# The second shift's row tiles: from TensorE to ScalarE and GpSimd

## The reference

```
mod = c @ w_ada + b_ada                      # w_ada: 2048 x 12288
sh1, sc1, gt1, sh2, sc2, gt2 = split(mod, 6)
h    = rmsnorm(x, g_mix) * (1 + sc1) + sh1
proj = h @ w_in                              # 2048 x 5376; attention and retention on its columns
x    = x + gt1 * (concat(attention, retention) @ w_out)
h2   = rmsnorm(x, g_ffn) * (1 + sc2) + sh2
x    = x + gt2 * (square(relu(h2 @ w1)) @ w2)
out  = rmsnorm(x, g_final)
```

## Time and profile before

| | us |
|---|---|
| median of 3 runs | 1198.6 (1196.89 to 1198.94) |
| the profiled execution | 1198.73 |
| its span in the trace | 1196.9 |
| TensorE busy | 1128.5 (94%) |
| VectorE busy | 808.2 (68%) |
| ScalarE busy | 490.6 (41%) |
| GpSimd busy | 19.1 (2%) |

### The profile page before, as it was taken

One profiled execution on the slowest core, in us unless ns is written; L12 is line 12 of the kernel. 1 busy time (PEld: TensorE's weight loads), 2 busy tenths in 40 slices (PEclk: granted clock), 3 DMA queues, 4 the chain that ended last, 5 costly groups with the idle time before them and its releaser, 6 DMA issues.

```text
span 1196.9 us, 15614 instructions
## 1 busy us (share of the span) xinstructions
PE 1128.5 (94%) x6235; PEld 963.2 (80%) x6235; DVE 808.2 (68%) x653; ACT 490.6 (41%) x495; POOL 19.1 (2%) x23
## 2 busy tenths in 40 slices
PE   0489999999999999999999999999999999999996
PEld 0489989888778778888888888888888888888884
DVE  5877767988776978875656566655656555665675
ACT  2233444554543445444333444333444333444442
POOL 2000001000000000100000000000000000000000
PEclk9779999999999999999999999999999999999998
DMA  9999988899997866767666667666666665665541
GB/s 363 402 331 332 361 295 296 317 363 385 354 407 298 293 218 234 233 189 266 225 235 187 186 190 255 239 217 200 185 205 245 217 240 182 188 194 182 190 155 71
DMA packets 152250, 302.94 MB, mean 253 GB/s; under 512 B 5088, under 2 KB 73296, under 8 KB 143632
## 3 DMA queue, kind: packets, MB, share of 16 engines
q1 hardware_dynamic: 150880, 298.08, 71.4%
q10 hardware_dynamic: 832, 2.93, 0.6%
q0 software_dynamic: 496, 1.35, 0.3%
HBM read 300.24 MB, written 2.10 MB: 253 GB/s over the span
## 4 chain that ended last, share of the span: by engine, by line
PE 87%; DVE 8%; DMA 3%; issue 1%; ACT 0%; ACTq 0%; DVEq 0%; SPq 0%
PE ps_job L765 18%; PE ps_job L800 14%; PE ps_job L802 14%; PE ps_job L801 14%; PE ps_job L768 9%; PE ps_job L780 4%; PE ps_job L781 4%; PE ps_job L782 4%; DVE acc L1045 3%; DVE w_lo L1105 2%; PE ps L864 1%; DMA stage<-in_w_ada 1%; DMA gate_rows<-in_w_ada 1%; PE ps L742 1%; DMA cst<-in_consts 1%
## 5 line engine op out<-in xcount | busy, mean ns | idle before, releaser
L1105 DVE TENSOR_TENSOR w_lo<-stage,w_hi 128x2048 fp32r<-128x2048 f32 x186 | 426.2, 2291 | 244.2 <-ACT w_hi L453 244.1
L453 ACT ACTIVATE w_hi<-stage 128x2048 fp32r<-128x2048 f32 x186 | 356.1, 1915 | 512.4 <-PE ps_job L802 309.4
L765 PE MATMUL ps_job<-act_hl,w_hi 128*128 128x512 f32 x1024 | 322.2, 396 | 2.3 <-DVE w_lo L1105 1.6
L768 PEld LDWEIGHTS ps_job<-act_hl,w_lo 128*128 128x128 f32 x1024 | 192.4, 188 | 45.4
L768 PE MATMUL ps_job<-act_hl,w_lo 128*128 128x256 f32 x1024 | 201.2, 278 | 0.0
L800 PE MATMUL ps_job<-w_hi,hid_hl 128*128 128x512 f32 x512 | 200.8, 392 | 0.0
L801 PE MATMUL ps_job<-w_lo,hid_hl 128*128 128x512 f32 x512 | 199.3, 389 | 0.0
L802 PE MATMUL ps_job<-w_hi,hid_hl 128*128 128x512 f32 x512 | 199.2, 389 | 0.0
L765 PEld LDWEIGHTS ps_job<-act_hl,w_hi 128*128 128x128 f32 x1024 | 156.1, 189 | 3.3 <-issue 1.8
L1045 DVE SCALAR_TENSOR_TENSOR acc<-stage,small,acc 128x2048 f32<-128x2048 f32 x64 | 150.3, 2348 | 5.7 <-DMA stage<-in_w_ada 2.6
L801 PEld LDWEIGHTS ps_job<-w_lo,hid_hl 128*128 128x128 f32 x512 | 96.1, 188 | 20.8 <-issue 1.0
(11 more groups left out here) (170 smaller groups left out, 788.4 us busy)
## 6 DMA issues: line engine op xcount, KB each, us to landing
stage<-in_w SPq DMA_DIRECT2D x128, 1024.0 KB, 5.4
stage<-in_w_ada SPq DMA_DIRECT2D x80, 1024.0 KB, 7.2
stage<-in_w_in SPq DMA_DIRECT2D x42, 1024.0 KB, 6.3
stage<-in_w_out SPq DMA_DIRECT2D x16, 1024.0 KB, 8.4
gate_rows<-in_w_ada SPq DMA_DIRECT2D x16, 1024.0 KB, 7.1
x_sb<-in_x ACTq DMA_DIRECT2D x1, 2048.0 KB, 14.2
out_y<-f_acc SPq DMA_DIRECT2D x3, 512.0 KB, 4.3
acc<-in_g_final POOLq DMA_DIRECT2D x1, 1024.0 KB, 7.4
```

Of the source, the lines that this page charges most:

```text
L453: nc.scalar.activation(w_hi[:, ring, :], stage[:, slot, :], ACT.Copy).then_inc(hi_ready, 1)
L765: nc.tensor.matmul(ps_job[:, 2 * pair + e, :], w_hi[:, ring, ws], act_hl[:, kt, :], start=(kt == 0), stop=False)
L768: last = nc.tensor.matmul(ps_job[:, 2 * pair + e, T:2 * T], w_lo[:, ring, ws], act_hl[:, kt, 0:T], start=False, stop=(kt == KT - 1))
L1105: nc.vector.tensor_tensor(w_lo[:, ring, :], stage[:, slot, :], w_hi[:, ring, :].bitcast(F32), ALU.subtract).then_inc(lo_ready, 1)
```

## The change

The row tiles no longer pass through TensorE one pair at a time. For each, ScalarE multiplies the tile in place in its slot by its values of c (`scale_row`, an ACTIVATE of 128x2048), and GpSimd adds the slot to an accumulator of its own, `row_acc` (a TENSOR_TENSOR of 128x2048, both inputs in SBUF). `scale_row` stands in ScalarE's program right ahead of the rounding of the group that follows the row tile. After g55 TensorE sums `row_acc` over its rows as it sums the others, with 16 matmuls.

The row tiles move in the list: before, two stood ahead of g29, g31, and so on to g43; now one stands ahead of each of g23, 24, 26, 28, 30, 32, 33, 35, 37, 39, 41, 42, 44, 46, 48 and 50. They are called r0 to r15 below. They count in `lo_ready` no more: a slot that held a row tile is free when GpSimd has added it (`row_added`), and SyncE waits for that.

```diff
-PRE = 5 * KT
+PRE = 4 * KT
+ROW_GROUP = [G_B + 4 + (G_MLP - G_B - 10) * k // KT for k in range(KT)]
...
-    if _g - 2 in [values_group(b) for b in range(PAIRS)]:
-        ITEMS += [("row", _g - 2 - values_group(0)), ("row", _g - 1 - values_group(0))]
+    if _g in ROW_GROUP:
+        ITEMS.append(("row", ROW_GROUP.index(_g)))
...
+READY = [sum(what != "row" for what, _ in ITEMS[:i + 1]) for i in range(len(ITEMS))]
... SyncE
-                load_group(src, i % SLOTS, i - SLOTS + 1)
+                before = i - SLOTS
+                if before >= 0 and ITEMS[before][0] == "row":
+                    sp.wait_ge(row_added, ITEMS[before][1] + 1)
+                load_group(src, i % SLOTS, READY[before] if before >= 0 else 0)
... GpSimd
             start_sum(0)
+            start_sum(1)
             pool.wait_ge(act_ready, 4)
-            for n in range(STRIPS):
-                pool.dma_start(rows[32 * n:32 * n + 32, :], b_ada[0:1, SH2 + TOK_COLS * n:SH2 + TOK_COLS * (n + 1)].to_broadcast([32, TOK_COLS])
-                               ).then_inc(rows_loaded, 16)
-            start_sum(1)
+            nc.gpsimd.memset(row_acc[:, :], 0.0).then_inc(row_zeroed, 1)
+            pool.wait_ge(row_zeroed, 1)
+            pool.dma_start(row_acc[0:1, :], b_ada[0:1, SH2:SH2 + D]).then_inc(row_bias_loaded, 16)
+            pool.wait_ge(row_bias_loaded, 16)
+            for k in range(KT):
+                if k:
+                    pool.wait_ge(row_added, k)
+                pool.wait_ge(row_scaled, k + 1)
+                nc.gpsimd.tensor_tensor(row_acc[:, :], row_acc[:, :], stage[:, ITEM_OF_ROW[k] % SLOTS, :], ALU.add).then_inc(row_added, 1)
             start_sum(2)
... ScalarE
+            def scale_row(k):
+
+                item = ITEM_OF_ROW[k]
+                act.wait_ge(stage_full[item % SLOTS], 16 * (item // SLOTS + 1))
+                nc.scalar.activation(stage[:, item % SLOTS, :], stage[:, item % SLOTS, :], ACT.Copy,
+                                     scale=vec_T[:, V_C + k:V_C + k + 1]).then_inc(row_scaled, 1)
...
+                    if g in ROW_GROUP:
+                        scale_row(ROW_GROUP.index(g))
                     if g >= 2:
                         static_group(g)
... TensorE
-            def row_sums(b):
-            def turn_rows():
...
+                    if g == G_MLP - 3:
+                        pe.wait_ge(row_added, KT)
+                        sum_mod(row_acc[:, :], 2, 0)
...
                         probs_values(pair_at(g, 6))
-                        row_sums(pair_at(g, 6))
...
-            turn_rows()
... VectorE
-            def add_rows(b):
...
-                        elif g and ITEMS[i][1] % 2:
-                            add_rows(ITEMS[i][1] // 2)
```

More of the change, by code:

```diff
@@ L82 @@
 SUM_FROM = 18
-PRE = 5 * KT
-def values_group(b):
-    return FIRST[J_BQ] + 7 + 2 * b
+PRE = 4 * KT
+ROW_GROUP = [G_B + 4 + (G_MLP - G_B - 10) * k // KT for k in range(KT)]
 def tiles_before(g):
@@ L146, in build @@
         y_part = sb("y_part", [P, TT, D], F32, y_at + 16384)
-        rows = sb("rows", [P, TOK_COLS], F32, y_at + 8192)
+        row_acc = sb("row_acc", [P, D], F32, y_at + 8192)
         h2_T = sb("h2_T", [P, KT, T], F32, y_at)
@@ L230, in build @@
         x_normed = sem("x_normed")
-        rows_loaded, rows_summed = map(sem, ("rows_loaded", "rows_summed"))
+        row_zeroed, row_bias_loaded, row_scaled, row_added = map(sem, ("row_zeroed", "row_bias_loaded", "row_scaled", "row_added"))
         first_rows_done = sem("first_rows_done")
@@ L345, in load_gate_rows @@
                 else:
-                    sp.wait_ge(lo_ready, len(ITEMS))
+                    sp.wait_ge(lo_ready, READY[-1])
                 sp.dma_start(gate_rows[:, m % 2, :], w_ada[0, m * P:(m + 1) * P, GT2:GT2 + D]).then_inc(gate_rows_full[m % 2], 16)
@@ L737, in turn_second, with sum_mod @@
                 last.then_inc(turned, 1)
-            def sum_mod(a, bank, col):
+            def sum_mod(source, bank, col):
                 for k in range(KT):
-                    last = nc.tensor.matmul(ps[:, bank, col + k:col + k + 1], acc[:, a, k * P:(k + 1) * P], ones[:, 0:1], start=True, stop=True)
+                    last = nc.tensor.matmul(ps[:, bank, col + k:col + k + 1], source[:, k * P:(k + 1) * P], ones[:, 0:1], start=True, stop=True)
                 last.then_inc(mod_summed, 1)
@@ L746, in _ @@
             pe.wait_ge(turned_out, 8)
-            pe.wait_ge(lo_ready, ITEM_OF_TILE[KT - 1] + 1)
-            sum_mod(0, 0, 0)
+            pe.wait_ge(lo_ready, READY[ITEM_OF_TILE[KT - 1]])
+            sum_mod(acc[:, 0, :], 0, 0)
             def half_feature_group(j, k0, ring):
@@ L836, in turn_probs @@
                     pe.wait_ge(att_ready, b)
-                    pe.wait_ge(lo_ready, ITEM_OF_ROW[2 * b - 1] + 1)
                 for e in range(2):
@@ L906, in _ @@
                     g = FIRST[j] + q
-                    pe.wait_ge(lo_ready, ITEM_OF_GROUP[g] + 1)
+                    pe.wait_ge(lo_ready, READY[ITEM_OF_GROUP[g]])
                     if q == 0 and jobs_out_before(j):
@@ L926, in _ @@
                     if g == G_B - 2:
-                        pe.wait_ge(lo_ready, ITEM_OF_TILE[2 * KT - 1] + 1)
-                        sum_mod(1, 2, 0)
+                        pe.wait_ge(lo_ready, READY[ITEM_OF_TILE[2 * KT - 1]])
+                        sum_mod(acc[:, 1, :], 2, 0)
+                    if g == G_MLP - 3:
+                        pe.wait_ge(row_added, KT)
+                        sum_mod(row_acc[:, :], 2, 0)
                     if g == G_B + 1:
@@ L939, in _ @@
                         pe.wait_ge(att_ready, PAIRS)
-                        pe.wait_ge(lo_ready, ITEM_OF_ROW[KT - 1] + 1)
                         for h in range(RET_HEADS):
@@ L954, in _ @@
                             pe.wait_ge(ret_ready, 2 * RET_HEADS)
-                            pe.wait_ge(lo_ready, ITEM_OF_TILE[3 * KT - 1] + 1)
+                            pe.wait_ge(lo_ready, READY[ITEM_OF_TILE[3 * KT - 1]])
                         if n >= 2:
@@ L960, in _ @@
             PB = J_MLP % 2
-            turn_rows()
-            pe.wait_ge(lo_ready, ITEM_OF_TILE[4 * KT - 1] + 1)
-            sum_mod(0, 3, 0)
+            pe.wait_ge(lo_ready, READY[ITEM_OF_TILE[4 * KT - 1]])
+            sum_mod(acc[:, 0, :], 3, 0)
             for r in range(4):
@@ L1041, in sum_tile @@
                 if k:
-                    dve.wait_ge(lo_ready, item)
+                    dve.wait_ge(lo_ready, READY[item] - 1)
                 else:
```

## The result

The changed kernel takes 1219.9 us (median of 4 runs, 1218.5 to 1222.1), the kernel before 1198.4 beside it: 1.0186 times as long, 95% interval 1.0173 to 1.02. The forecast was 1216, slower. The profiled execution took 1218.5 us with a span of 1216.5, against 1198.7 and 1196.9: 19.6 us more of span, and these I account for (the medians lie 21.5 us apart).

A forecast was written before the change was run, and what follows sets the result against it. The prediction took TensorE to bound A, B and C, with VectorE near and the bound in D. Delays of 8.6 (start of g42), 4.6 (D) and 4.2 (E) gave 17.4 on 1198.7, so 1216 us, range 1191 to 1232.

The forecast's parts named there:

- A: Stretch of r0 to r3, from g23: holds make VectorE 9.4 us late, less a 4.4 us lead, TensorE +5.0.
- D: Stretch of r14 and r15, where VectorE is the bound: their additions delay column sums by 1.6 and 3.0 us, +4.6.
- B: Stretch of r4 to r11: VectorE 3.9 us later, 13.3 in all, and decides the start of g42, +8.6.
- E: Last stretch, to the projection's end: 16 new TensorE matmuls on `row_acc` behind g55, +4.2 us.
- The addition's length: GpSimd's addition of a row tile: 4.5 us taken, bounds 1.8 and 5.4.
- The hold: Each GpSimd addition keeps VectorE from instructions with two SBUF inputs: 3.4 us taken, the middle of 2.3 to 4.5.
- Rival 1: No hold: GpSimd and VectorE read side by side, TensorE stays the bound, -10.6, about 1189 us; chance 0.20.
- The bound of 2.3: Lower hold per 4.5 us addition, VectorE using about 2.2 us for work with at most one large SBUF input; 1203 us.
- The term of the pairs: TensorE loses eight pairs of row tiles at 1.85 us: 14.8 us go, 12.95 between the starts of g29 and g42.
- C: Stretch of r12 and r13: VectorE is busy 21.4 of 33.8 us and waits for TensorE, so 0.
- Rival 2: GpSimd's additions wait for VectorE's gaps, row tiles stay in `stage`, loads come late: 1204 us; chance 0.10.
- Rival 3: A short hold of 1.9 to 2.3 us, most additions starting just behind a split: 1199 to 1203 us; chance 0.12.

The follow-up runs named there:

- experiment 1: The changed kernel without the 16 GpSimd additions, ScalarE still scaling each row tile: 1187.4 us, 0.9916 of the kernel before.
- experiment 2: The changed kernel with GpSimd memsets, which only write, in place of each addition, GpSimd busy about as long: 1190.3 us, 0.9942 of the kernel before.
- experiment 3: The changed kernel with a one-input GpSimd multiplication of row_acc by 1.0 in place of each addition: 1205.6 us, 1.0071 of the kernel before.
- Experiment 9: The changed kernel with GpSimd adding only r0 to r3, the others scaled but left out of the sum: 1202.6 us, 1.0047 of the kernel before.
- experiment 11: The kernel before without the pairs' 64 matmuls, a tiny instruction replacing VectorE's addition of their sums: 1189.5 us, 0.9937 of the kernel before.
- experiment 7: The kernel before with 16 more one-column matmuls behind g55, result unused: 1201.9 us, 1.0043 of the kernel before.
- experiment 4: The changed kernel without ScalarE's 16 scalings, the rows added unscaled: 1222.8 us, 1.0208 of the kernel before.

## Why the prediction was right

The mechanism was right, the forecast 3.9 us low (1216 against 1219.9). That it came so near is partly luck: A was put 7.0 us too low and D 1.6, B 3.0 and E 3.4 too high. By its steps, how much later TensorE is than before (profiled executions; starts of the same matmul):

| at | predicted | measured |
|---|---|---|
| g29 | +5.0 | 262.4 - 250.4 = +12.0 |
| g42 | +8.6 | 366.1 - 353.6 = +12.6 |
| g50 | +13.2 | 431.45 - 412.65 = +18.8 |
| end of the projection | +17.4 | +19.6 |

**The addition's length**: taken at 4.5 us; undisturbed ones take 4.54 to 4.63. Right. The figure of the Trainium skill (GPSIMD Engine Reference, section 3.1), 4497 ns, agrees.

**The hold**: 3.4 us an addition, the middle of 2.3 and 4.5; measured 3.2 on average. Rival 1 is refuted by the rows above and experiment 1, and experiment 2 shows why were silent: memsets don't hold. The bound of 2.3 rested on VectorE going on under the logits (L1140, L1149). It does, but tiny instructions between them are held for up to 4.4 us, as L1150 shows. The rule of the Trainium skill (SBUF — State Buffer, section "SBUF: two separate sides"), exclusion for the whole instruction, is what these rows show for the additions; experiment 3 departs from it, where VectorE went on 1.9 us before GpSimd's TENSOR_SCALAR ended. Besides two SBUF inputs against a GpSimd read, that section names a VectorE operation in a two-port performance mode as one that takes the pair. L1190 and L1171, TENSOR_SCALARs with one SBUF tensor, are held too; whether they ran in such a mode no run here shows.

**A** is the mis-sized term: +5.0 predicted, +12.0 measured. The sum counted 13.6 us of holds less 4.2 of slack less a lead of 4.4. The holds were 16.5 us (4.38, 4.34, 3.32 and 4.41), which gives 7.9 by the same arithmetic. For the other 4.1 I see two causes, which no run separates. The lead is that of the splits, but the scores need `q_T`, which VectorE writes just before TensorE reads it: this wait has no lead, and it took 6.17 us. And the clock was at 0.92 in A, some 0.08 x 32.2 = 2.6 us of TensorE's busy time. Counted on TensorE itself, it waits 10.2 us before it takes up g29 (6.17, 2.70, 1.00 and 0.30) and loses 2.7 to the clock, and one pair of 1.85 is gone: 11.0 of the 12.0. Experiment 9 shows that A's additions cost 15.2 us even with nothing behind them: none of it is won back.

**B**: +3.6 predicted, +0.6 measured. Its eight additions held VectorE 23.8 us, not 27.2. TensorE waited 9.4 us between g29 and g42, in four waits; with 3.1 us for the slower clock that is 12.5, nearly the 12.95 us of the pairs. That VectorE decides there holds (101.9 of 102.9 busy): its split of g42 ends at 363.14 + 2.28 = 365.4, 0.7 us before TensorE takes it up, where the lead was 4.7. The term of the pairs has its own limit, which I had not seen: where the row tiles stay in B it is worth 8.0 us (experiment 11), since the loads become the limit there. In the changed kernel, where they are spread, the full sum without a hold came about (-10 by the ratio of experiment 1).

**C and D**: 0 and +4.6 predicted, +6.2 together measured. C came out free: the split of g46 starts 12.6 us late (395.27 against 382.71), as late as TensorE at g42. In D the excess of the last two additions is 3.44 + 2.80 us, the same 6.2, so the mechanism was right and the two holds were put 1.6 us too short.

**E**: +4.2 predicted, +0.8 measured. The sum itself takes 3.6 us, and experiment 7 puts it at +5.0 in the kernel before. It was hidden in part, by the clock of the kernel before in the stretch of the wait behind g52. Before, then after:

```profile
428.00:440.00 12.00, 9.91 (x36) 7.62 (x36) 9.11 (x6) 3.85 (x6) 0.00 (x0) 0.86 0.51 155
```

```profile
447.00:459.00 12.00, 9.91 (x42) 7.54 (x41) 10.69 (x7) 5.34 (x7) 0.00 (x0) 1.00 0.63 207
```

Both wait for the same split for 2.1 us, but only before did the clock fall, which cost 1.6 us there (0.27 x 3.44 + 0.16 x 4, in windows of 4 us). `turn_rows` (0.95 us), for which the prediction counted nothing, went as well. 3.6 - 1.6 - 0.95 = 1.1 is near the 0.8 measured.

**ScalarE** costs nothing (experiment 4), as said. **Rival 2** did not come: the additions start when their scaling is done, all 16 (ScalarE's L472 ends every idle time before one in GpSimd's timeline), and ScalarE, where a late slot would show, waits less for loads than before: 8.6 us between 204.9 and 475 against 17.4.

**Rival 3** needed holds of 1.9 to 2.3 us; they were 3.2 on average.

As a whole, up to the end of the projection: waits of TensorE +22.4 us (26.3 - 3.9), the new sum less the pairs and `turn_rows` 3.6 - 15.8 = -12.2, together +10.2. For the clock I summed TensorE's busy time times what the granted clock lacked of full, in windows of 4 us from 204 us to 464 before and to 484 after: 1.6 and 8.7, so +7.1. That is 17.3 of the 19.6; 2.3 us I can't place. The prediction did not price the clock at all.

## What to carry to other kernels

An idle engine is not free if it reads the same memory as a busy one: price the instruction by the time that it takes from its neighbour (here 3.2 us for 2.35 us' worth of work), and do the work on the neighbour if that is less. A lead of one buffer covers only waits for that buffer; look for short steps between two engines that have none, and keep holds away from them. A long wait on TensorE (here 3.6 us and more) costs its length and then a stretch at the lower clock.

## What the runs showed of the hardware

- GpSimd's addition, which reads SBUF, and many VectorE instructions with SBUF inputs follow each other, whichever began first. Held were instructions from 128x2048 down to 128x4, of two SBUF tensors, and TENSOR_SCALARs of one (L1190, 4.06 us, and L1171 at 128x8, 1.88). A TENSOR_REDUCE of one SBUF tensor ran on (L1139, 1.01 us for two during an addition), and so did instructions with a tensor in PSUM (L1184, 0.87 us for two, once VectorE's split was over and the addition had begun).
- GpSimd's memset, which only writes, held nothing (column sum 2.34 us beside it). Its TENSOR_SCALAR, which reads one tensor, held a column sum for 3.4 of its 5.37 us.
- GpSimd's TENSOR_SCALAR of 128x2048 in float32 takes 5.37 us, its TENSOR_TENSOR 4.54, its MEMSET 1.81.
- The granted clock was at 0.50 to 0.57 in the window of 4 us behind waits of 3.65, 3.80 and 6.17 us. Behind one of 2.70 us it stayed at 1.00 (240 to 244). Behind a wait of 2.1 us it fell in one kernel (428 to 440, 0.86) and not in the other (447 to 459, 1.00).
